# A three-block kernel: the borders of the second block, its weight stream and its convolution stage

## The reference, cut to what matters

```python
def second_block(x, norm_gain, w_in, conv_dw_w, ..., final_gain):
    h = _rmsnorm_2(x, norm_gain[l])
    proj = jnp.einsum('bsd,de->bse', h, w_in[l])
    a_val, a_glu, a_gate, q, k, v, r_gate, g_a, g_b = jnp.split(proj, SPLIT_POINTS, axis=-1)
    u = a_val * jax.nn.sigmoid(a_glu)
    u = lax.conv_general_dilated(u, conv_dw_w[l][:, None, :], ..., feature_group_count=CONV_CH) + conv_dw_b[l]
    u = jax.nn.silu(_layernorm(u, conv_ln_g[l], conv_ln_b[l]))
    u = u * jax.nn.silu(a_gate)
    y_a = jnp.einsum('bsc,cd->bsd', u, w_conv_proj[l])
    ...                      # rotary q and k, chunked retention, head norm, times silu(r_gate) -> o
    y_b = jnp.einsum('bsc,cd->bsd', o, w_ret_proj[l])
    m = jax.nn.sigmoid(g_a) * y_a + jax.nn.sigmoid(g_b) * y_b
    x = x + jnp.einsum('bsd,de->bse', m, w_out[l])
    return _rmsnorm_2(x, final_gain)
```

## Time and profile before

| | us |
|---|---|
| median of 3 runs | 5464.95 (5461.77 to 5467.32) |
| profiled execution | 5470.23 |
| its span | 5468.5 |
| PE busy | 4801.5 (88%) |
| DVE busy | 2447.2 (45%) |
| POOL busy | 1262.5 (23%) |
| ACT busy | 1168.8 (21%) |

### The profile page before, as it was taken

How to read it: one execution, slowest core, us unless ns; L and a number is a source line. 1 busy time by engine, 2 the same in 40 slices (tenths; PEclk the granted TensorE clock), 3 DMA queues, 4 the chain that set the end, 5 groups by cost and what they waited for, 6 DMA issues and landing times. The chain is left out here.

```text
span 5468.5 us, 57841 instructions
## 1 busy us (share of the span) xinstructions
PE 4801.5 (88%) x22844; PEld 3746.1 (69%) x22844; DVE 2447.2 (45%) x2430; ACT 1168.8 (21%) x1396; POOL 1262.5 (23%) x616
## 2 busy tenths in 40 slices
PE   5999888859999998975897699999999899997877
PEld 4888776638787786853676587777778566665556
DVE  6454554441312212999443532424242344446853
ACT  3322321121111111111201211212121122224420
POOL 1222112102222131454121222213222111111221
PEclk7999997879999999987998889999998999998988
DMA  2111212111111111101230201101010111115441
GB/s 101 53 58 50 76 63 105 54 62 43 66 35 70 39 66 62 42 23 66 95 116 31 84 27 38 39 23 60 19 58 14 72 60 59 56 45 204 166 162 46
DMA packets 110977, 356.59 MB, mean 65 GB/s; under 512 B 12404, under 2 KB 13956, under 8 KB 110664
## 3 DMA queue, kind: packets, MB, share of 16 engines
q1 hardware_dynamic: 81952, 292.95, 15.5%
q10 hardware_dynamic: 28840, 60.91, 2.9%
HBM read 263.43 MB, written 90.39 MB: 65 GB/s over the span
## 5 line engine op out<-in xcount | busy, mean ns | idle before, releaser
L546 POOL CAST b_w_hi<-b_w 128x1024 fp32r<-128x1024 f32 x157 | 180.9, 1152 | 2487.5 <-PE ps L610 1910.6
L610 PE MATMUL ps<-h_hT_hi,b_w_hi 128*128 128x512 f32 x1216 | 521.5, 429 | 27.9 <-PEq L95 24.5
L610 PE MATMUL ps<-h_hT_lo,b_w_hi 128*128 128x512 f32 x1216 | 491.5, 404 | 0.0
L610 PE MATMUL ps<-h_hT_hi,b_w_lo 128*128 128x512 f32 x1216 | 489.9, 403 | 0.0
L548 POOL TENSOR_TENSOR b_w_lo<-b_w,b_w_hi 128x1024 fp32r<-128x1024 f32 x157 | 416.3, 2652 | 12.6
L610 PE MATMUL ps<-b_hT_hi,b_w_hi 128*128 128x512 f32 x848 | 357.2, 421 | 55.0 <-PEq L95 19.9
L610 PE MATMUL ps<-b_hT_lo,b_w_hi 128*128 128x512 f32 x848 | 342.3, 404 | 0.0
L610 PE MATMUL ps<-b_hT_hi,b_w_lo 128*128 128x512 f32 x848 | 341.7, 403 | 0.0
L478 PE MATMUL ps<-b_hi,ret_w_hi 128*128 128x512 f32 x768 | 301.1, 392 | 29.6 <-DVE ret_w_lo L445 29.6
L610 PEld LDWEIGHTS ps<-h_hT_hi,b_w_hi 128*128 128x128 f32 x1216 | 235.7, 194 | 127.6 <-issue 72.0
L478 PE MATMUL ps<-b_lo,ret_w_hi 128*128 128x512 f32 x768 | 299.4, 390 | 0.0
(11 more groups left out here) (649 smaller groups left out, 10074.2 us busy)
## 6 DMA issues: line engine op xcount, KB each, us to landing
b_w<-in_w SPq DMA_DIRECT2D x157, 512.0 KB, 3.4
ret_w<-in_w SPq DMA_DIRECT2D x64, 512.0 KB, 3.3
scratch_x_park<-xT SPq DMA_DIRECT2D x24, 512.0 KB, 7.8
conv_w<-in_w SPq DMA_DIRECT2D x24, 512.0 KB, 3.3
xT<-scratch_x_park SPq DMA_DIRECT2D x16, 512.0 KB, 8.8
scratch_gate_park<-ret_gates_out ACTq DMA_DIRECT2D x16, 512.0 KB, 2.7
scratch_o_park<-ret_o ACTq DMA_DIRECT2D x16, 512.0 KB, 5.7
scratch_gate_park<-rw_fill_out ACTq DMA_DIRECT2D x32, 256.0 KB, 2.0
```

Source lines behind the costliest of these rows:

```text
L546: pool.tensor_copy(hi, w).then_inc(self.rounded, 1)
L610: ins = pe.matmul(out[:, t], w, y, start=start, stop=stop)
```

## The change

- **Norms at a border from two sums.** A new class `TokenScales` runs inside the last projection of block 1 (`narrow_projection`) and of block 2 (`stream_projection`, argument `border`). With s1 = 1/sqrt(mean(x²)+eps), both norms together are x*g1*s1*g2*s2, where s2 needs only the mean of g1²x². ACT squares each tile as it is added, DVE keeps the two sums, PE adds them over partitions by one-column matmuls and ACT and DVE turn them into both scales. SP stores the tile that isn't normalised to `x_park`. The stages fin1, rms2, fin2 and rms3 are gone.
- **`norm_and_first_tile`** applies both scales at once, splits h (even tiles' rest on DVE, odd ones' on POOL) and multiplies the next block's first weight tile in the same stage.
- **`Residual`** normalises the parked x where it is read back: in "ya" (now `gated_projection`) and in `joined_projection`.
- **One weight stream for block 2.** `SplitProjection`, `Filler`, `GatedProjection`, `OutProjection` and `weighted_projection` are removed; all tiles of block 2 lie in one tensor `w2` and run through one `Stream`, so that a stage's first tile is loaded and split in the one before. The retention's fill tiles are evacuated by halves with `Fill`; the last unit multiplies the first convolution tile.
- **`conv_and_projection`** takes the place of `conv_branch` and `conv_end_and_projection`: 24 + 8 tiles written out, four PSUM pairs, a ring of four pads, eight convolutions on DVE, the product on POOL, the gate stored to `conv_park` and read back in the norm stage.

The core of the diff; new functions as they stand.

```diff
+class TokenScales:
...
+    def square(self, act, e, added):
+        act.wait_ge(added, e + 1)
+        if e >= 3:
+            act.wait_ge(self.summed, e - 1)
+        dst = self.sq[:, e % 2, :] if e else self.acc[:, 0, :]
+        act.activation(dst, self.x[:, e, :], ACT.Square).then_inc(self.squared, 1)
...
+            dve.tensor_tensor(acc[:, 0, :], acc[:, 0, :], sq, ALU.add)
+            dve.scalar_tensor_tensor(acc[:, 1, :], sq, g, acc[:, 1, :], ALU.mult, ALU.add).then_inc(self.summed, 1)
...
+    def add_up(self, pe):
+        pe.wait_ge(self.summed, KD - 1)
+        for n in range(2):
+            for c in range(NCH):
+                ins = pe.matmul(self.sums[:, n, c:c + 1], self.acc[:, n, c * C:c * C + C], self.core.mean_d[:, 0:1],
+                                start=True, stop=True)
...
+        pe.wait_ge(self.squared, KD)
+        for c in range(NCH):
+            ins = pe.matmul(self.rest[:, c, :], self.sq[:, (KD - 1) % 2, c * C:c * C + C], self.last[:, :],
+                            start=True, stop=True)
```

```diff
+def norm_and_first_tile(core, name, x, halves, stream, out, parked, loads=()):
...
+        @block.gpsimd
+        def _(pool):
+            stream.cut_tile(pool, 0)
+            for k in range(1, KD, 2):
+                cut_h(pool, k)
...
+            ins.then_inc(spread_done, 1)
+            stream.multiply(pe, out, 0, y_cut=cut)
...
+            spread_tokens(dve, diag[:, :, :], core.ident[:, :], core.scales[:, 1, :]).then_inc(spread_ready, 1)
+            dve.wait_ge(spread_done, 1)
+            for k in range(KD):
+                if k >= ring:
+                    dve.wait_ge(cut[k % 2], (k - ring) // 2 + 1)
+                dve.scalar_tensor_tensor(h[:, k % ring, :], x[:, k, :], core.gains[:, 1, k:k + 1], scale, ALU.mult, ALU.mult) \
+                    .then_inc(normed, 1)
+                if k % 2:
+                    cut_h(dve, k - 1)
...
+class Residual:
...
+    def apply(self, dve, k):
+        if k == 0:
+            dve.wait_ge(self.spread_done, 1)
+        x = self.x[:, k, :]
+        dve.scalar_tensor_tensor(x, x, self.core.col(self.gain, k), self.scale, ALU.mult, ALU.mult)
```

```diff
-def conv_branch(core, wt, first, halves, pads, uT, gate):
-def conv_end_and_projection(core, pads, uT, *projection):
+def conv_and_projection(core, stream, first_tile, base, uT, conv_park, o_dram, gates, mixed):
...
+        @block.gpsimd
+        def _(pool):
+            pool.wait_ge(padded, 1)
+            for u in range(KD):
+                for t in range(nt):
+                    stream.cut_tile(pool, first_tile + 1 + nt * u + t)
+                pool.wait_ge(evacuated, nt * u + 2)
+                if u >= ring:
+                    pool.wait_ge(conv_done, u - ring + 1)
+                pool.tensor_tensor(pads[:, u % ring, CW - 1:], val[:, :], sig[:, :], ALU.mult).then_inc(multiplied, 1)
+            for k in range(KD):
+                if k == KD // 2:
+                    stream.cut_tile(pool, base + 1)
+                pool.wait_ge(y_rounded, k + 1)
+                pool.tensor_tensor(stream.y_lo[:, k, :], mixed[:, k, :], stream.y_hi[:, k, :], ALU.subtract).then_inc(y_cut, 1)
+            for e in range(1, KD):
+                stream.cut_tile(pool, base + 1 + e)
...
+        @block.vector
+        def _(dve):
...
+            for u in range(KD):
+                dve.wait_ge(multiplied, u + 1)
+                if u == KD - 1:
+                    for e in range(2):
+                        dve.wait_ge(y_cut, KD)
+                        add(dve, e, bank(e), mixed, False, gated, added)
+                    conv(u, 0, CW // 2)
+                    for e in range(2, 4):
+                        add(dve, e, bank(e), mixed, False, gated, added)
+                    conv(u, CW // 2, CW)
+                else:
+                    conv(u, 0, CW)
```

782 lines of the change are left out of this document (339 added, 443 removed).

## The result

| | before | after |
|---|---|---|
| median, us | 5466.14 (5461.77 to 5476.67, 4 runs) | 5368.05 (5357.28 to 5374.38, 4 runs) |
| ratio | | 0.9819, 95% interval 0.9801 to 0.9837 |
| profiled execution, us | 5470.23, span 5468.5 | 5357.28, span 5355.5 |
| PE busy in it | 4801.5 | 4788.8 |
| DVE busy | 2447.2 | 2458.1 |

The change is 98 us faster by the medians, 115 were forecast. The profiled execution is the fastest of the four, and by the two traces alone the gain is 113.0 us. The trace of after by stretch, with the columns of the earlier trace rows: the first border from the last matmul of block 1 to the start of weight tile 1, the retention, the merged convolution stage, the norm stage, the second border.

The account below looks back on a forecast made before the run. Waits at the block borders and DVE, last to end in the convolution stages, were taken as bounds; 48+42-6+30+6-2.7+1.9-4.3 = 115 us off 5470.2 gives 5355, less 5.3: 5350 us, range 5318 to 5415.

Parts of the forecast that it names:

- 7.3+31+5+1.7+2 = 47: First border after: end of sums, new stage, barrier and cut, lower clock, lag; 47 us in place of 94.9.
- the lag of 2 us: First border: allowance of 2 us because DVE's sums beside the last projection were hidden only closely.
- The "46" for the second border: Border of blocks 2 and 3: 46 us after, by the first border's sum without the lag, from 87.6.
- four units of +1.5: Retention: variance matmuls wait some 5 us where 3.7 stood, in each of four units; 6 us lost (0 to 12).
- DVE ends at 452, and the stage some 4 us later: Merged convolution stage: DVE's chain sets the end, stage 456 us in place of 487.7, 30 us gained.
- PE needs 338, and hides: Merged convolution stage: PE's 31 tiles of 10.9 us take 338 us and stay hidden behind DVE.
- rival (a): Merged stage: a third of 28 casts held some 20 us, stage 525 us, total 5419; chance 0.10.
- Rival (b): Merged stage: every second or third cast waits for DVE's chain to break, stage 600 us, total 5494; chance 0.03.
- Rival (d): Borders give less: cutting engines take turns, PE stays at 1.2 GHz, 15 us each, total 5380; chance 0.20.
- Rival (c): Merged stage: POOL's stalls of DVE lighter than priced, gain 55 us in place of 30, total 5325; chance 0.17.
- The rule of the Trainium skill: Merged stage: two-input DVE and SBUF-reading GpSimd instructions exclude each other, whoever starts first; stalls 131 us in place of 119.
- The rest: Other stages: norm stage 6 us gained, ya 2.7 lost, o2 1.9 gained, block 3's joined projection 4.3 lost.

Follow-up runs that it names:

- after_again: The changed kernel once more, unaltered, for a second trace; median 5366.43 us, ratio 0.9824.
- v3: Changed kernel with weight loads before gate loads, fill half behind squares, adds forward, merged-stage rounding on ACT, ACT's store wait moved; median 5354.59 us.
- sp_order: Changed kernel with weight loads ahead of gate loads in SP's queue in the merged convolution stage; median 5351.99 us, ratio 0.9789.
- copy_cut: Changed kernel with POOL copying 24 weight tiles where it subtracted, so results are wrong; four runs from 5356.97 to 5452.3 us.
- act_round: Changed kernel with the merged stage's weights rounded on ACT and only subtracted on POOL; median 5373.84 us, ratio 0.983.
- v4: Changed kernel with weight loads before gate loads, fill half behind squares, adds forward, ACT's store wait moved, input subtractions on DVE; median 5320.73 us.
- v5: v4 with every sixth DVE multiplication of a convolution waiting for its direct predecessor; median 5314.9 us, ratio 0.9728.

## Why the prediction held, and where it didn't

The range (5318 to 5415 around 5350 us) holds the measured 5368, and the sign is right. By its own steps:

- **Borders.** 53.7 and 46.0 us gained, forecast 48 and 42; both within their bounds. The mechanism is the one described. The sum 7.3+31+5+1.7+2 = 47 was 41.2: the lag of 2 us beside the last projection was none (DVE's last sums end ahead of the last add), and most of tile 0 ran at the higher clock, from 1145.1 us on, where I had its last matmuls at half. In after_again it rose only at 1156.8, and the same way took 1.7 us longer. Granted were 0.78 and 0.69 over the two borders, in place of 0.52 and 0.57 in the earlier trace rows. The "46" for the second border is a slip: 47 without the lag of 2 is 45; measured were 41.6.
- **Retention.** The 5 us ahead of the variance matmuls came as worked out (5.02 in each unit), against 3.75 before. The step that failed is "four units of +1.5": it left out a gap of 2.05 to 2.29 us at each of the three turns of PE's loop, where the branch takes 6 us in place of 3.5 (v3), and the start of the stretch at the lower clock, 5.9 us of it from 1163.1 us on, where tile 1 before ran at the higher one. The four gaps are 5.1 us of loss, the turns 6.5 and the clock 3: 14.6 us, above the bound of 12.
- **The convolution stage.** The step that failed is "DVE ends at 452, and the stage some 4 us later", with "PE needs 338, and hides". DVE's last convolution and adds of that chain were done at 2557.9, 438 us into the stage; the stalls were about 104 us (101.5 of them the multiplications') where I had summed 119. But the stage ended at 473, with PE's last tile. I had followed DVE's queue and POOL's and had not followed SP's: the gate load that waits for an add stands there ahead of the weights, and stopped PE for 76 us. sp_order shows it: PE's wait for a weight is gone with the two swapped, and the stage is 20.6 us shorter. A second part of the tail is the cast of 16.07 us at the end, of rival (a), which cost PE 15.02 us; sp_order moved it too, so the 20.6 us are not the queue's alone. Rival (a) had asked for nine such casts and one came.
- **Rival (b)** was given 3 in 100. In the kernel as it stands none of 8 runs came near its 5494 us. copy_cut and act_round show how near it is: the same loop with copies for the subtractions has a stage of 558 us in one run, and with the subtraction first on POOL six holds.
- **Rival (d)**, borders that give less, is refuted by both borders. **Rival (c)**, lighter stalls, is true for 15 of the 25 us by which it had the stalls lighter, and the stage didn't get them, since its end was set elsewhere.
- **The rule of the Trainium skill** (SBUF — State Buffer, "Who interferes with whom") gave 131 us for the stalls, my rows 119, the chip 104. The rule that an instruction of DVE with two SBUF inputs and one of GpSimd that reads SBUF exclude each other agrees in kind with the pair of 2.06 and 3.41 us, in which a subtraction of 2.40 cost DVE 2.92. What it says of the order, that whoever comes first gets the ports and the other waits for the whole instruction, doesn't agree: a cast waited for some twenty-four DVE instructions (30.72 us), and a cast inside the chain, which reads SBUF too, cost DVE's multiplications nothing.
- **The rest.** The norm stage (5.2 for 6) came as forecast. ya and o2 together cost 1.3 us for 0.8. yssd lost 1.3 us for 4.3, and o3 2.4 that the forecast didn't have. The store of x, costed at nothing, ended none of PE's waits at the two borders: their rows name DVE and POOL only.
- **The sum.** 115 was forecast, the traces give 113.0, and that is an accident: 14.3 of them are the clock of that execution in code that is the same. The medians' 98 is the change, and that it lies within 17 of 115 is in part luck too: the convolution stage gave 17 less than its share and the retention 9 less, and the borders gave 10 more.

## What to carry to other kernels

Follow every queue that a merged stage writes out, the one that only issues loads too: a load that waits for a consumer stops all loads behind it, and the engine it starves may be three steps away. Where one engine runs a long chain without gaps and another one shares its ports, put a gap into the chain on purpose: a wait for the direct predecessor at every sixth instruction cost 0.6 us in 38 and took 29 us off a stage with six holds (act_round). In a stage with one long hold and time to spare on PE it took 3.6 us (v4 to v5), and the runs spread over 7.6 us in place of 13.7. When a norm stands between two projections, its sums can be made beside the first one; here two such borders gave 100 us, as much as the whole change.
